# One decoder step on one core: the sample heads laid over all partitions, and the decode attention's order rewritten

## The reference, cut

```python
proj = rmsnorm(x) @ w_in            # hq hf hi hg | mq mk mv, 512 columns each
# HGRN2, 4 heads of 128: f = lb + (1-lb)*sigmoid(hf), k = 1-f, q = silu(hq)
S_t = diag(f_t) @ S_{t-1} + outer(k_t, i_t);  o_t = S_t.T @ q_t
head = rmsnorm_head(o) * silu(hg)
# MoBA, 8 heads of 64: softmax attention with ALiBi; the prompt over its own keys, each sample
# over 4 gathered pages of 128 past keys and values (page_table) and its own 4 tokens
x += concat(head, moba) @ w_out
x += cross_attention_4heads(rmsnorm(x), K/V of rmsnorm(mem) or the cached ones)
x += hierarchical_moe(rmsnorm(x))   # 32 experts, top 2 in the best of 4 groups
y = rmsnorm_final(x)
```

## Time and profile before

| | |
|---|---|
| median of 3 runs | 1800.04 us (1799.89 to 1801.58) |
| the profiled execution | 1797.82 us, span 1795.8 us |
| TensorE matmul / load busy | 1479.6 us (82%) / 656.9 us (37%) |
| VectorE / ScalarE busy | 520.7 us (29%) / 272.4 us (15%) |
| granted TensorE clock, mean | 0.93 |
| moved by DMA | 522 MB, 291 GB/s over the span |

### The profile page before, as it was taken

The page is one execution under the profiler, slowest core; times in us unless marked ns, Lnnn a source line. Parts: engine busy times, 40 slices in busy tenths (PEclk is TensorE's granted clock), DMA queues, the critical chain, the costliest instruction groups (busy, mean ns, idle before and its releaser), DMA issues.

```text
span 1795.8 us, 18424 instructions
## 1 busy us (share of the span) xinstructions
PE 1479.6 (82%) x7041; PEld 656.9 (37%) x7041; DVE 520.7 (29%) x1012; ACT 272.4 (15%) x607; POOL 95.8 (5%) x106
## 2 busy tenths in 40 slices
PE   6999989985898989959878787878888787878790
PEld 3445554563344555443322222222222222222220
DVE  3065775451222142252212121212111121212125
ACT  2113325431111131110000000000000000000002
POOL 3000000000000000000000000000000000000002
PEclk9999989987899999969999999999989898999995
DMA  8911311328731236359999999999999999999984
GB/s 290 339 49 51 115 48 60 128 79 275 282 137 59 94 107 253 140 190 413 421 421 422 421 422 421 422 421 422 421 421 421 421 422 421 421 422 422 421 343 168
DMA packets 103703, 522.02 MB, mean 291 GB/s; under 512 B 11506, under 2 KB 12066, under 8 KB 54496
## 3 DMA queue, kind: packets, MB, share of 16 engines
q1 hardware_dynamic: 85760, 468.48, 64.4%
q0 software_dynamic: 14768, 45.97, 7.5%
q10 hardware_dynamic: 3120, 6.82, 1.0%
HBM read 496.97 MB, written 32.11 MB: 295 GB/s over the span
## 4 chain that ended last, share of the span: by engine, by line
DMA 45%; PE 42%; DVE 9%; ACT 1%; issue 1%; SPq 1%; POOL 0%; ACTq 0%; DVEq 0%; POOLq 0%
DMA ring<-w 43%; PE psum L1939 10%; PE psum L2418 8%; PE psum L1927 7%; PE psum L2025 3%; PE psum L2441 2%; PE psum L1912 1%; DVE ring L1392 1%; PE psum L2274 1%; PE psum L2297 1%; DMA ring<-w_in 1%; PE psum L2155 1%; PE psum L2053 1%; SPq L581 1%; PE psum L2131 1%
## 5 line engine op out<-in xcount | busy, mean ns | idle before, releaser
L2418 PE MATMUL psum<-ring,r_c 128*64 128x512 f32 x1536 | 394.7, 665 | 133.5 <-DMA ring<-w 132.5
L2441 PE MATMUL psum<-ring,r_c 128*64 128x512 f32 x1024 | 233.4, 598 | 49.2 <-DMA ring<-w 36.8
L2418 PEld LDWEIGHTS psum<-ring,r_c 128*64 128x64 f32 x1536 | 121.0, 151 | 403.4 <-DMA ring<-w 220.1
L1842 DVE TENSOR_SCALAR r_c<-r_c 128x512 f32<-128x512 f32 x32 | 13.7, 427 | 761.4 <-ACT r_c L1182 761.4
L2441 PEld LDWEIGHTS psum<-ring,r_c 128*64 128x64 f32 x1024 | 73.0, 136 | 187.5 <-issue 91.2
L1927 PE MATMUL psum<-r_h,ring 128*128 128x512 f32 x320 | 138.8, 594 | 0.0
L1939 PE MATMUL psum<-ring,r_h 128*128 128x512 f32 x256 | 114.8, 608 | 3.8 <-DMA ring<-w_in 3.8
L1182 ACT ACTIVATE r_c<-psum 128x512 f32<-128x512 f32 x32 | 19.1, 597 | 615.8 <-PE psum L2418 615.8
L1844 DVE RECIPROCAL r_c<-r_c 128x512 f32<-128x512 f32 x32 | 107.3, 3353 | 1.1
L1927 PEld LDWEIGHTS psum<-r_h,ring 128*128 128x128 f32 x320 | 60.5, 191 | 75.3 <-issue 75.3
L779 POOL DMA_INDIRECT out_rows<-r_c,maskd x32 | 31.6, 988 | 903.5 <-ACT r_c L1192 903.5
(11 more groups left out here) (353 smaller groups left out, 1369.6 us busy)
## 6 DMA issues: line engine op xcount, KB each, us to landing
ring<-w SPq DMA_DIRECT2D x320, 1024.0 KB, 27.1
r_h<-w SPq DMA_DIRECT2D x32, 1024.0 KB, 26.1
r_mix<-w SPq DMA_DIRECT2D x32, 1024.0 KB, 26.2
ring<-w_in SPq DMA_DIRECT2D x7, 2048.0 KB, 10.5
out_rows<-zeros POOLq DMA_DIRECT2D x3, 4096.0 KB, 18.3
ring<-cache_mem_k POOLq DMA_DIRECT2D x8, 1024.0 KB, 7.5
ring<-cache_mem_v SPq DMA_DIRECT2D x8, 1024.0 KB, 10.0
ring<-cache_moba_v SPq DMA_DIRECT2D x24, 256.0 KB, 6.3
```

The lines of the kernel that those rows point to most:

```text
L2418: ins = pe.matmul(psum[2 + 2 * u + m][CAP * half:CAP * (half + 1), :], xT[:, k, CAP * u:CAP * (u + 1)], moe_place(2 * q + m, u)[:, kk, 512 ...
L2441: ins = pe.matmul(psum[7][CAP * half:CAP * (half + 1), :], heT[u][:, k % 4, CAP * (k // 4):CAP * (k // 4 + 1)], ring[:, 8 + q, kk, 512 * h ...
```

## The change

- Everything of the sample heads that had 32 partitions by 512 columns (keys `kds`, values `vhs`, gates `ghs`, weights `atts`, head output) now has 128 partitions by 128 columns: head h sits in partitions 32h to 32h+31. The four-part copies become one instruction.
- `o(NT)`: one product of `atts` (block diagonal over the heads) with `vhs`, then for each sample four matmuls that go to the four strips in turn.
- `Us`: instead of masked keys, masked values `vhx` (two tensor products over 128 partitions). Eight matmuls of 32x128 by 512 columns, one for each head and half of the samples.
- The state updates stand in pairs between the key turnings, and the turning of the heads after key turnings 0 and 1.
- `mem_job(3, 1)` joins `MEM_STEP` at head 7.
- `qxm` has a place of its own and is filled in head preparation, behind `weights_inside(1)`.
- Buffers: the third key place moves to `TAIL + 4096` (`mv`), `kT` to `KV`, two value places to `TAIL`. SP: keys 1 wait for the last prompt scores, keys 2 for the last prompt values, value pages 0 follow keys 4 and the turned prompt heads. GpSimd loads the memory keys only when the second sample output is filled.

```diff
-MEM_STEP = [(0, 0), (0, 1), (1, 0), (1, 1), (2, 0), (2, 1), (3, 0)]
+MEM_STEP = [(0, 0), (0, 1), (1, 0), (1, 1), (2, 0), (2, 1), (3, 0), (3, 1)]
...
-    all_of("V", "Us", range(NB))
-    mem_job(3, 1)
-    all_of("A", "hgT")
 
     def keys_turned(what, b):
         for c in range(4):
             add("AV"[c % 2], what, b, c)
 
-    for b in range(4):
-        keys_turned("KT", b)
+    keys_turned("KT", 0)
+    all_of("A", "hgT", range(NT))
+    keys_turned("KT", 1)
+    add("A", "hgT", NT)
+    all_of("V", "Us", (0, 1))
+    keys_turned("KT", 2)
+    all_of("V", "Us", (2, 3))
+    keys_turned("KT", 3)
     add("V", "Sn", 0)
+    all_of("V", "Us", (4, 5))
     keys_turned("KT", 4)
+    all_of("V", "Us", (6, 7))
     keys_turned("KT", 5)
     add("A", "Pt", 0)
     add("V", "Ptn", 0)
...
-        vh = part(flat, TAIL, 5, 512)
-        gh = part(flat, TAIL + 2560, 5, 512)
-        mv = part(flat, TAIL + 5120, NT, 512)
-        kds = part(flat, TAIL + 7168, 512)
+        vh = part(flat, TAIL, NT, 512)
+        gh = part(flat, TAIL + 2048, NT, 512)
+        mv = part(flat, TAIL + 4096, NT, 512)
+        vhs = part(flat, TAIL + 6144, HD)
+        ghs = part(flat, TAIL + 6144 + HD, HD)
+        kds = part(flat, TAIL + 6144 + 2 * HD, HD)
...
-        kdx = part(flat, KV, NB, 512)
+        vhx = [part(r_c, (12 + n) * TOK, 4, HD) for n in range(2)]
...
-        kbuf = [part(r_h, 0, NPG, 512), part(r_c, 8 * TOK, NPG, 512), part(r_x, 0, NPG, 512)]
-        vbuf = [part(flat, KV + 2048 * n, NPG, 512) for n in range(3)] + [part(r_h, 4 * TOK, NPG, 512)]
-        kT = [part(flat, TAIL + 2048 * n, 4, PAST) for n in range(2)]
+        kbuf = [part(r_h, 0, NPG, 512), part(r_c, 8 * TOK, NPG, 512), part(flat, TAIL + 4096, NPG, 512)]
+        vbuf = [part(flat, TAIL, NPG, 512), part(flat, TAIL + 2048, NPG, 512), part(flat, KV + 4096, NPG, 512),
+                part(r_h, 4 * TOK, NPG, 512)]
+        kT = [part(flat, KV + 2048 * n, 4, PAST) for n in range(2)]
...
-        qxm = part(flat, TAIL + 6144, 4, NB, 32)
+        qxm = part(flat, TAIL + 7168, 4, NB, 32)
...
             sp.wait_ge(qx_done, 1)
+            J.wait_filled(sp, "S", MB - 1, NT - 1)
             key_pages(1)
-            J.wait_filled(sp, "mem", 3, 1)
-            sp.wait_ge(out_mem, 32)
-            value_pages(0)
-            sp.wait_ge(out_s0, 16)
+            J.wait_filled(sp, "OT", 3)
+            sp.wait_ge(out_mv, 32)
             key_pages(2)
             for b in range(3, 8):
                 J.wait_filled(sp, "KT", b - 3, 3)
                 key_pages(b)
+                if b == 4:
+                    J.wait_filled(sp, "hgT", NT - 1)
+                    sp.wait_ge(out_mem, 32)
+                    value_pages(0)
...
-            J.wait_emptied(pool, "Us", NB - 1)
+            J.wait_emptied(pool, "Us", 7)
...
-            pool.wait_ge(sc_full, NB // 2)
+            J.wait_filled(pool, "Os", 1)
...
-                if i < NT:
-                    ins = act.activation(gh[:, i, :], J.bank("hg", i), ACT.Exp, scale=-1.0)
-                else:
-                    for n in range(4):
-                        ins = act.activation(gh[0:NS, i, P * n:P * (n + 1)], J.bank("hg", i)[NS * n:NS * (n + 1), 0:P],
-                                             ACT.Exp, scale=-1.0)
-                ins.then_inc(exped, 1)
+                out, src = (gh[:, i, :], J.bank("hg", i)) if i < NT else (ghs, J.bank("hg", i)[:, 0:P])
+                act.activation(out, src, ACT.Exp, scale=-1.0).then_inc(exped, 1)
...
-                evac(kds[0:NS, HD * h:HD * (h + 1)], "kds", h, view=lambda s: s[0:NS, 0:HD])
+            evac(kds, "kds", view=lambda s: s[:, 0:HD])
...
-            for i0, i1, r in ((0, NT, P), (NT, NT + 1, NS)):
-                if i0 == NT:
-                    head_squares(NT)
-                J.wait_emptied(act, "o", i1 - 1)
-                act.activation(hy0[0:r, i0:i1, :], hss[0:r, i0:i1, :], ACT.Sqrt, scale=1.0 / HD, bias=EPS)\
-                    .then_inc(o_root, 1)
-
+            J.wait_emptied(act, "o", NT - 1)
+            act.activation(hy0[:, 0:NT, :], hss[:, 0:NT, :], ACT.Sqrt, scale=1.0 / HD, bias=EPS).then_inc(o_root, 1)
+            head_squares(NT)
+            J.wait_emptied(act, "o", NT)
+            act.activation(hy0[:, NT, 0:1], hss[:, NT, 0:1], ACT.Sqrt, scale=1.0 / HD, bias=EPS).then_inc(o_root, 1)
             act.wait_ge(out_mem, 16)
-            for i, _ in TILES:
-                turn_heads(i)
...
-            for b in range(4):
-                keys_turned(b)
+            keys_turned(0)
+            for i in range(NT):
+                turn_heads(i)
+            keys_turned(1)
+            turn_heads(NT)
+            keys_turned(2)
+            keys_turned(3)
...
             def gated(i):
 
-                r = rows(i)
                 dve.wait_ge(exped, 6 + i)
-                g = gh[0:r, i, :]
+                g = gh[:, i, :] if i < NT else ghs
                 v(dve.tensor_scalar(g, g, 1.0, None, ALU.add))
                 v(dve.reciprocal(g, g))
+                J.empties(dve.tensor_tensor(g, J.bank("hg", i)[:, 0:(HG if i < NT else 1) * HD], g, ALU.mult), "hg", i)
+                J.wait_emptied(dve, "hg", i)
                 if i < NT:
-                    ins = dve.tensor_tensor(g, J.bank("hg", i)[0:r, :], g, ALU.mult)
+                    g3 = g.rearrange("p (h v) -> p h v", h=HG)
+                    st.did(dve.tensor_tensor(g3, g3, ghn[:, :].unsqueeze(1).to_broadcast([P, HG, HD]), ALU.mult))
                 else:
-                    for n in range(4):
-                        c = slice(P * n, P * (n + 1))
-                        ins = dve.tensor_tensor(g[:, c], J.bank("hg", i)[NS * n:NS * (n + 1), 0:P], g[:, c], ALU.mult)
-                J.empties(ins, "hg", i)
-                J.wait_emptied(dve, "hg", i)
-                g3 = g.rearrange("p (h v) -> p h v", h=HG)
-                st.did(dve.tensor_tensor(g3, g3, ghn[0:r, :].unsqueeze(1).to_broadcast([r, HG, HD]), ALU.mult))
+                    st.did(dve.tensor_tensor(g, g, ghn[:, :], ALU.mult))
+
...
                 weights_inside(h)
+                if h == 1:
+                    sample_queries_apart()
                 if h == 2:
                     gated(4)
...
+            def heads_normed():
+
+                dve.wait_ge(o_root, 1)
+                y = refined(hy0[:, 0:NT, :], hss[:, 0:NT, :], HD, [hnt[:, k, 0:NT, :] for k in range(3)], HG)
+                for i in range(NT):
+                    g = gh[:, i, :].rearrange("p (h v) -> p h v", h=HG)
+                    dve.tensor_tensor(g, g, y[:, i, :].unsqueeze(2).to_broadcast([P, HG, HD]), ALU.mult)\
                         .then_inc(heads_done, 1)
+
+            def sample_heads_normed():
+
+                dve.wait_ge(o_root, 2)
+                y = refined(hy0[:, NT, 0:1], hss[:, NT, 0:1], HD, [hnt[:, k, NT, 0:1] for k in range(3)], 1)
+                dve.tensor_scalar(ghs, ghs, y, None, ALU.mult).then_inc(heads_done, 1)
...
-            J.wait_filled(dve, "OT", 3)
-            J.wait_emptied(dve, "kds", HG - 1)
-            for b in range(NB):
-                ins = dve.tensor_scalar(kdx[0:NS, b, :], kds[0:NS, :], bsel[:, b:b + 1], None, ALU.mult)
+            J.wait_filled(dve, "S", MB - 1, NT - 1)
+            J.wait_emptied(dve, "hi", NT)
+            for n in range(2):
+                ins = dve.tensor_tensor(vhx[n], vhs.unsqueeze(1).to_broadcast([P, 4, HD]),
+                                        bsel[:, 4 * n:4 * n + 4].unsqueeze(2).to_broadcast([P, 4, HD]), ALU.mult)
             ins.then_inc(qkx_done, 1)
-            v(dve.memset(qxm.rearrange("p a b c -> p (a b c)"), 0.0))
-            for h in range(MB):
-                par, c = h % 2, h // 2
-                rr = slice(64 * par, 64 * par + 64)
-                ins = dve.tensor_copy(qxm[rr, c, :, NQ * h:NQ * (h + 1)],
-                                      mqT[rr, c, SEQ:TOK].rearrange("p (b t) -> p b t", t=NQ))
-            ins.then_inc(qx_done, 1)
-            heads_normed(0, NT, P)
+            heads_normed()
             gate_applied(NT)
-            heads_normed(NT, NT + 1, NS)
-            for b in range(NB):
-                J.wait_filled(dve, "Us", b)
-                for h in range(HG):
-                    u = J.bank("Us", b)[:, HD * h:HD * (h + 1)]
+
+            def sample_states(n):
+                half, h = n // HG, n % HG
+                J.wait_filled(dve, "Us", n)
+                for b in range(4 * half, 4 * half + 4):
                     ins = dve.scalar_tensor_tensor(out=s0[:, b, h, :], in0=s0[:, b, h, :],
-                                                   scalar=dl[:, h, NCH + b:NCH + b + 1], in1=u,
+                                                   scalar=dl[:, h, NCH + b:NCH + b + 1],
+                                                   in1=J.bank("Us", n)[:, HD * (b % 4):HD * (b % 4 + 1)],
                                                    op0=ALU.mult, op1=ALU.add)
-                J.empties(ins, "Us", b)
-
-
```

(66 more changed lines are left out.)

62 lines of the change are left out of this document (33 added, 29 removed).

## The result

The changed kernel takes 1767.35 us (median of 4 runs, 1766.54 to 1768.05) against 1799.97 us (4 runs, 1794.97 to 1801.58): ratio 0.982, 95% interval 0.9804 to 0.9836. The forecast was 1763.5 us, in a range of 1755 to 1778. The profiled execution took 1767.24 us, span 1765.1; that of before 1797.82, span 1795.8. So 30.7 us of span are to be accounted for.

A forecast was written before the change was run, and what follows sets the result against it. The chain ahead of the experts' weight stream was taken to set the time. 3.9 + 5.4 + 30.2 - 3.0 = 36.5 off the profiled 1797.8 gives 1761.3, plus 2.2 for the median: 1763.5 us, range 1755 to 1778.

The forecast's parts named there:

- Gated(4): Sample rows' gates on VectorE, ahead of head 3: as 128 rows of 128, 5.6 us become 1.7, saving 3.9.
- The early clock: TensorE behind the idle before head 3: with that idle cut to 2.5 us the clock stays up, saving 5.4.
- the early clock falls anyway: Rival: 2.5 us of idling before head 3 still drops the clock, 5.4 stays lost: 1769 us, chance 0.20.
- The middle stretch: 372 to 463 us, head 7's scores to the first sample output's end, laid out anew: 30.2 us less.
- clock charge of 3: TensorE behind its new idle from 386 us: half clock for about 8 us, costing 3, bounds 0 and 10.
- What follows is the same work.: Behind the first sample output nothing was to change, and the second value pages were to lose a competitor.
- What would show it: Signs: gated(4) below 2 us, full clock 248 to 260, memory product 7, first output ending near 427, experts' stream 36 earlier.
- the first rival: The clock before head 3 falls despite the shorter idle, 5.4 us stays lost: 1769 us, chance 0.20.
- a half clock throughout: Rival: TensorE at half clock through most of 389 to 427 us, 13 us more: 1777, chance 0.12.
- a half stall left: Rival: keys 2 or 5 land late behind other transfers, half of the 17.33 us stall stays: 1772, chance 0.06.
- the slower case: Rival: value pages leave later; landing 46 us late loses the gain, at 50 it is 1804 us; chance 0.03.
- the third: Rival: late keys 2 or 5 leave half of TensorE's 17.33 us wait for key pages: 1772 us, chance 0.06.

The follow-up runs named there:

- e7: The changed kernel with one more unused VectorE reciprocal (3.35 us) behind the sample rows' gate, making it as long as before: 1775.54 us, ratio 0.9866.
- e4: The changed kernel with three idle products in TensorE's gap ahead of head 3's small products: 1764.23 us, ratio 0.9808.
- e8: The changed kernel with SP's queue in the old order, the first value pages ahead of keys 2: 1780.08 us, ratio 0.9891.
- e12: The changed kernel with the last dense memory product back behind the sample heads instead of beside head 7, a repeat of e6: 1776.38 us, ratio 0.9867.
- e5: The changed kernel with the sample heads' loops swapped, all eight samples of one column strip before the next: 1770.72 us, ratio 0.9827.
- e10: The kernel of e9 with five more idle products, three before the sample heads and two before their turning: 1757.27 us, ratio 0.9766.
- e1: The changed kernel storing only the first sample's new state, 256 KB instead of 2 MB: 1763.02 us, ratio 0.9809.
- e2: The changed kernel with the prompt rows' 2 MB load waiting until all value pages have landed: 1760.92 us, ratio 0.9799.
- e9: The changed kernel with three idle products ahead of head 3 and the prompt rows loaded behind all value pages: 1761.5 us, ratio 0.9784.
- e3: The changed kernel with all four pairs of state products and updates ahead of key turning 2: 1768.95 us, ratio 0.9824.
- e11: The changed kernel run once more, unedited, as the reference for e9, e10 and e12: 1769.87 us, ratio 0.9835 to the kernel before.
- e6: The changed kernel with the last dense memory product back behind the sample heads instead of beside head 7: 1773.65 us, ratio 0.9851.

## Why the prediction was right, and where a step was not

The number held: 32.6 us between the medians where 36.5 were forecast. The spans of the profiled executions differ by 30.7, as that of before lay 2.15 us below its median. Step by step in them:

- **Gated(4).** 229.60 to 235.24 before, 230.79 to 232.58 after: 3.85 saved, 3.9 predicted. The queries set apart cost nothing: VectorE still idles 5.43 us behind them. e7 confirms the place: 3.35 us put back there start head 3 some 2.9 us later (251.94, against 249.36 and 248.74).
- **The early clock.** 5.4 predicted, 2.06 measured: this step failed. The idle shrank to 2.85 us, about the 2.5 predicted, and the clock fell after it nonetheless, for some seven microseconds. The rival "the early clock falls anyway" was right in the mechanism, though it held all 5.4 to be lost. My inference made a threshold of one event, and read it wrongly: 0.83 over the microsecond from 249 puts the fall at 249.7, 4.1 us into the old idle and not 3.6. The traces with the same short gap lost between 3.15 and 6.0 us against e4's 8.01, so even the 2.06 is partly chance. e4 shows the lost part, with the gap filled.
- **The middle stretch.** Predicted 30.2 less a clock charge of 3, so 27.2. From the end of head 7's scores to the end of the first output it was 91.08 us and is 59.96 (367.62 to 427.58): 31.1. To the first output, e8 gives 10.75 of it to keys 2 in SP's queue and e12 8.4 to the product's place; e5 gives the strips 0.8 as the traces stand and 4.0 at equal clock; the rest was not isolated. Too dear in my sum were the states' products, 1.8 a pair by the long records, measured 1.13 at full clock (2.08 at half), and the first output, 6.2 taken and 4.59 measured, which is the clock's chance named above. Too cheap were the sample heads, 2.1 taken and 3.17 measured, partly at half clock. The clock charge of 3 was sound in size: the clock was at half in parts of 384 to 402, and e10, which kept it up there, is 3.7 us shorter to the first output's start and 2.0 to its end (42.62 against 44.66), which is where my sum ended. There e1, e2, e7 and e9 have 44.53 to 44.59 too, and only e4 less, 43.14. A wrong reason beside a right number: I let the memory product delay the state's store and so the sample heads, by 4.1 us. They started 15.3 us after head 7's scores, where I had 16.6, but e12 shows that the product has no part in that delay.
- **"What follows is the same work."** This is the other step that failed: 0 predicted, 6.84 us lost between key turning 6 and the projection. I counted the transfer that leaves the neighbourhood of the second value pages, the memory keys, and not those that arrive. The pages are now asked for from 427.71, 5.9 us behind the states' store (421.77), with the prompt's rows behind them (435.74). Both transfers were in the diff's reach, since the state updates and POOL's waits moved. e1 and e2 show that the pages' part, 5.4 us from output to output, takes both. The rest of the 6.84 is the clock's fall that had left the first output, less 0.2 that came back behind the second.
- **The start and the end.** Gated(4) starts 1.19 us later than before, 0.9 of it from the first weights' wait (4.09, before 3.76) and the first matmuls (9.26, before 8.72), which the diff doesn't touch; the stream behind the projection is 1.70 shorter. I take both for chance.
- **What would show it.** The first output ends at 427.58, near 427 as said, gated(4) takes 1.79 us and the memory product 7.13; TensorE waits for no key pages. Two signs failed: the clock was at half from 251 to 258, and the projection comes 29.0 us earlier (the experts' first products 29), not 36.

The sum: 3.85 + 2.06 - 1.19 + 31.12 - 6.84 + 1.70 = 30.7. The two terms that failed, -3.3 and -6.8, stood against a stretch 3.9 better than predicted. That the errors had opposite signs is luck, and the 1767.35 measured lies nearer to the first rival's 1769 than to the forecast of 1763.5. Of the other rivals, a half clock throughout (1.00 over 402 to 438), a half stall left and the slower case did not occur. e8 prices what the third would cost in whole: 10.75.

## What to carry to other kernels

When a store or a load is moved, look in the timeline for the transfers that will now run beside it, those that arrive as well as those that leave: a stall that is cleared lets the same megabytes meet the next batch of pages, and e3 shows that moving them earlier can do no more than choose which batch waits. A load with slack (here the prompt's rows) is best chained behind the pages that have none. Where short waits surround short matmuls, measure what the granted clock costs by filling the gap with idle products, before counting on a shorter gap to keep it. And before a difference of a few us between two traces is given to an edit, look at the granted clock in both: the same code took 36.85 to 40.07 us over one stretch here, and that hid four fifths of what the strips' turn-taking is worth.

## What the runs showed of the hardware

A gap of 2.85 us was followed by a fall of the clock two microseconds after it ended, while TensorE worked without a gap (0.57 from 251 to 252). Filled with three idle products, the gap was followed by no fall in e4 and e10, and by a shorter one in e9, among the turnings:

```profile
258.70 3.04 PE L2033 MATMUL psum<-ident,r_c 128*128 128x128 f32 x16
```

And the same code finds another clock from one execution to the next: over 145 to 165 us the changed kernel's profile has a mean granted clock of 0.91 and its repetition e11 1.00, those of e9 and e10, whose code does not differ there, 0.74 and 1.00 (e9's row, then e10's):

```profile
145.00:165.00 20.00, 19.60 (x60) 11.80 (x61) 7.29 (x12) 2.54 (x3) 0.00 (x0) 0.74 0.21 78
```

```profile
145.00:165.00 20.00, 20.00 (x71) 10.72 (x70) 11.67 (x21) 4.86 (x6) 0.00 (x0) 1.00 0.15 57
```

e9 then reaches head 3 at 254.83 us, against 248.9 in e10: 5.9 us, more than most single steps that are argued over here. e6's profile has 0.74 there too, and reaches head 3 at 252.83. What decides the clock there was not tested.
